# The pool groups of a two-layer decoder trunk: seven block products for eight in the looped groups, one weight sum by accumulating DMAs

## What is computed

```python
def pool_branch(xn, w_in, w_group, scale, w_out):
    u, g = jnp.split(xn @ w_in, 2, axis=-1)          # 2048 -> 2 x 4096
    for gi, w in enumerate((2, 4, 8, 16)):           # 4 groups of 1024 columns
        outs.append(windowed_mean(u[group gi], w) - u[group gi])
    mixed = einsum('bsgc,gce->bsge', stack(outs), w_group) * scale
    return (mixed * silu(g)) @ w_out                 # 4096 -> 2048
```

## Time and profile before

| what | value |
|---|---|
| median of the runs | 1543.48 us |
| profiled execution | 1544.08 us, its span 1542.0 us, granted clock 0.998 |
| busy in the span | PE 99%, DVE 72%, ACT 61%, POOL 2% |
| matmuls | 6788 records |
| DMA | 333.11 MB, 216 GB/s; queue of plain loads 60.7% and queue of POOL's DMAs 5.8% of 16 engines |

### The profile page before, as it was taken

The page is one execution under the profiler, slowest core; times in us unless marked ns, Lnnn a source line. Parts: engine busy times, 40 slices in busy tenths (PEclk is TensorE's granted clock), DMA queues, the critical chain, the costliest instruction groups (busy, mean ns, idle before and its releaser), DMA issues.

```text
span 1542.0 us, 19948 instructions
## 1 busy us (share of the span) xinstructions
PE 1525.7 (99%) x6788; PEld 1260.2 (82%) x6788; DVE 1114.2 (72%) x1382; ACT 935.8 (61%) x1124; POOL 28.9 (2%) x40
## 2 busy tenths in 40 slices
PE   9999999999999999999999999999999999999997
PEld 7887888888888888888888888888888888888885
DVE  6978787877878788887666675775577557755665
ACT  6466574657657574756777556644764476446853
POOL 0000000000000000000000000000000000000000
PEclk9999999999999999999999999999999999999999
DMA  9486786959678686965665757655765576555651
GB/s 382 167 257 222 223 239 218 244 171 276 220 217 244 218 219 223 242 224 198 223 220 187 219 211 219 217 196 191 218 219 189 194 221 228 210 208 180 223 195 72
DMA packets 137529, 333.11 MB, mean 216 GB/s; under 512 B 80992, under 2 KB 81008, under 8 KB 116368
## 3 DMA queue, kind: packets, MB, share of 16 engines
q1 hardware_dynamic: 132608, 314.35, 60.7%
q0 software_dynamic: 4736, 17.95, 5.8%
q10 hardware_dynamic: 144, 0.26, 0.0%
HBM read 312.08 MB, written 2.10 MB: 204 GB/s over the span
## 4 chain that ended last, share of the span: by engine, by line
PE 91%; DVE 3%; DMA 2%; issue 2%; ACT 2%; SPq 0%; ACTq 0%; POOL 0%; DVEq 0%; POOLq 0%
PE accA L515 11%; PE accA L517 11%; PE accA L516 11%; PE accC L515 10%; PE accC L517 10%; PE accC L516 10%; PE accB L515 6%; PE accB L517 6%; PE accB L516 6%; DMA w_raw<-in_stream_dram 2%; PE side L549 1%; PE side L548 1%; PE side L547 1%; DVE w_lo L1332 1%; PE accA L534 1%
## 5 line engine op out<-in xcount | busy, mean ns | idle before, releaser
L1332 DVE TENSOR_TENSOR w_lo<-w_raw,w_hi 128x1024 fp32r<-128x1024 f32 x326 | 395.8, 1222 | 226.3 <-ACT w_hi L861 224.6
L861 ACT CAST w_hi<-w_raw 128x1024 fp32r<-128x1024 f32 x326 | 340.0, 1052 | 263.2 <-PE accA L517 100.1
L1262 DVE TENSOR_TENSOR w_lo<-w_raw,w_hi 128x1024 fp32r<-128x1024 f32 (+1 forms) x280 | 320.9, 1167 | 95.4 <-ACT w_hi L874 95.4
L874 ACT CAST w_hi<-w_raw 128x1024 fp32r<-128x1024 f32 (+1 forms) x280 | 274.8, 1008 | 161.3 <-PE accA L517 79.4
L515 PE MATMUL accA<-w_hi,xa_hi 128*128 128x512 f32 x452 | 176.0, 389 | 0.8 <-DVE w_lo L1332 0.8
L517 PE MATMUL accA<-w_hi,xa_lo 128*128 128x512 f32 x452 | 175.9, 389 | 0.0
L516 PE MATMUL accA<-w_lo,xa_hi 128*128 128x512 f32 x452 | 175.9, 389 | 0.0
L515 PE MATMUL accC<-w_hi,xa_hi 128*128 128x512 f32 x396 | 154.3, 390 | 0.2 <-DVE w_lo L1262 0.2
L516 PE MATMUL accC<-w_lo,xa_hi 128*128 128x512 f32 x396 | 154.1, 389 | 0.0
L517 PE MATMUL accC<-w_hi,xa_lo 128*128 128x512 f32 x396 | 154.0, 389 | 0.0
L515 PEld LDWEIGHTS accA<-w_hi,xa_hi 128*128 128x128 f32 x452 | 84.8, 188 | 18.7 <-issue 1.1
(11 more groups left out here) (276 smaller groups left out, 2807.5 us busy)
## 6 DMA issues: line engine op xcount, KB each, us to landing
w_raw<-in_stream_dram SPq DMA_DIRECT2D x162, 1024.0 KB, 4.8
w_raw<-in_stream_dram SPq DMA_DIRECT2D x224, 512.0 KB, 5.5
w_raw<-in_stream_dram POOLq DMA_DIRECT2D x28, 512.0 KB, 8.6
h<-in_x_dram SPq DMA_DIRECT2D x4, 512.0 KB, 12.7
xT_raw<-in_xT_dram SPq DMA_DIRECT2D x3, 512.0 KB, 13.7
dec<-in_decay_dram POOLq DMA_DIRECT2D x1, 1024.0 KB, 9.1
fgain<-in_final_gain_dram POOLq DMA_DIRECT2D x1, 1024.0 KB, 7.5
out_dram<-emb SPq DMA_DIRECT2D x1, 1024.0 KB, 3.8
```

The lines of the kernel that those rows point to most:

```text
L861: act.copy(w_hi[:, r % RING, :], w_raw[:, r // 2, (r % 2) * 1024:(r % 2 + 1) * 1024]).then_inc(hi_ready, 1)
L874: act.copy(dst, unit_raw(name)).then_inc(hi_ready, 1)
L1262: dve.tensor_tensor(w_lo[:, u % RING, 0:n], unit_raw(ORDER[u]), w_hi[:, u % RING, 0:n].bitcast(F32), ALU.subtract).then_inc(lo_ready, 1)
L1332: dve.tensor_tensor(w_lo[:, r % RING, :], w_raw[:, r // 2, (r % 2) * 1024:(r % 2 + 1) * 1024], w_hi[:, r % RING, :].bitcast(F32), ALU.subt ...
```

## The change

In the looped groups, the first eight tiles of the two u products and of the two g products are done by the seven block products, with their own order (P_ORDER, 68 units: 40 whole ones and 28 parts), their own list of loads of 512 KB into named half-slots (P_LOADS), and the other work of ACT, DVE and SP at new places. u is the first pair, g the second. In pair u, T1 is made by DVE (pool_t1) and T3 by two accumulating DMAs; in pair g both T1 and T3 are made by accumulating DMAs. T2 and T4 are DVE's in both. POOL starts the sums of a group when the first turn's transposes have landed and T1 of u is there. The activation sums are made in group 0 (pool_form_sum, ACT's copies, pool_form_lo); f1 is written over a block of xa that is no longer used. In group 0 the two group products go to pairs B and C, not A and B, and the waits at the start of the last close change with them. The buffers of the snapshots and sums lie in parts of the arena and of other buffers. The stream is put in the order of the loads. Group 0 keeps its 40 units. The diff, cut to its core:

```diff
+P_ORDER = ("uA4 uM1a uA5 uM1b uA6 uM3a uA7 uM3b uC4 uM5a uC5 uM5b uC6 uM6a uC7 uM6b O0 uM7a O1 uM7b O2 uM4a O3 uM4b uM2a uM2b "
+           "O4 O5 O6 O7 O8 O9 O10 O11 O12 O13 O14 O15 gA4 gM1a gA5 gM1b gA6 gM3a gA7 gM3b gC4 gM5a gC5 gM5b gC6 gM6a "
+           "gC7 gM6b D0 gM7a D1 gM7b D2 gM4a D3 gM4b gM2a gM2b D4 D5 D6 D7").split()
...
+P_LOADS = (("uA4", 7, "uA4"), ("uX1a", 4, "uM4a"), ("uA5", 5, "uA5"), ("uX1b", 6, "uM4b"), ("uX2a", 2, "uM7a"), ("uA6", 0, "uA6"), ("uX3a",
+           1, "uM5b"), ("uA7", 3, "uA7"), ("uX2b", 7, "uM7b"), ("uX3b", 5, "uM6a"), ("uC4", 0, "uC4"), ("uC5", 3, "uC5"), ("uC6", 0, "uC6"),
+           ("uC7", 3, "uC7"), ("uX4a", 1, "uM2a"), ("uX4b", 0, "uM2b"), ("O0", 5, "O0"), ("O1", 3, "O1"), ("O2", 5, "O2"), ("O3", 2, "O3"),
+           ("O4", 3, "O4"), ("O5", 7, "O5"), ("O6", 5, "O6"), ("O7", 4, "O7"), ("O8", 2, "O8"), ("O9", 6, "O9"), ("O10", 1, "O10"), ("O11",
...
+P_TURNS = ('uX2b', 'uC6', 'O11', 'gA5')
...
+P_FORMS = (2, 0, 1, 3)
+FORM_SUM = (15, 33, 35, 36)
+FORM_HI = (17, 36, 38, 39)
+FORM_LO = (18, 37, 38, 39)
...
+            def group_loads(g, base):
+
+                last = {(POOL1 + r) % (2 * RAW): max(r, 1) - 2 * RAW for r in range(2 * RAW)}
+                for n, (name, b, last_name) in enumerate(P_LOADS):
+                    if name in P_TURNS:
+                        sp.wait_ge(halves_ready, g * 8 + (2 * POOL_TURNS - 4 + 2 * P_TURNS.index(name) + 2))
+                        sp.sem_inc(turn_begun, 1)
+                        transpose_halves(in_emb, halvesT_landed)
+                    sp.wait_ge(lo_ready, base + (last[b] + 1))
+                    last[b] = P_AT[last_name]
+                    at = g * (GROUP_U // (2 * RAW)) + ((POOL1 - GROUP_U + n) // (2 * RAW))
+                    s = (POOL1 + n) // 2 % RAW
+                    half = (POOL1 + n) % 2 * UNIT * COL
+                    sp.dma_start(slot(b), rounds[at, s, :, half:half + UNIT * COL]).then_inc(pool_landed[b], 16)
...
+            def add_pool_block(g, base, x, term, used):
+
+                n = POOL1 + [name for name, _slot, _last in P_LOADS].index(term)
+                at = (g - 1) * (GROUP_U // (2 * RAW)) + n // (2 * RAW)
+                half = n % 2 * UNIT * COL
+                pool.wait_ge(lo_ready, base + (P_AT[used] + 1))
+                pool.dma_start(slot(P_SLOT[x]), rounds[at, n // 2 % RAW, :, half:half + UNIT * COL],
+                               accum_op=ALU.add).then_inc(p_sum_landed[x], 16)
+
+            def group_sums(g, base, p):
+
+                if p == "g":
+                    add_pool_block(g, base, p + "X1a", p + "X2a", p + "M1a")
+                    add_pool_block(g, base, p + "X1b", p + "X2b", p + "M1b")
+                if p == "u":
+                    pool.wait_ge(p_t1_ready, g * 2)
+                wait_pool_landed(pool, g, p + "X2a")
+                add_pool_block(g, base, p + "X2a", p + "X3a", p + "M1b")
+                wait_pool_landed(pool, g, p + "X2b")
+                add_pool_block(g, base, p + "X2b", p + "X3b", p + "M1b")
...
+            for g in range(1, GROUPS):
+                base = g * GROUP_S + (POOL1 + MORE - GROUP_S)
+                pool.wait_ge(halvesT_landed, (POOL_TURNS + g * 4 - 1) * 16 * TT)
+                group_sums(g, base, "u")
+                group_sums(g, base, "g")
...
+            def pool_part(name, base, bank, hi, lo, first):
+
+                u = P_AT[name]
+                i = "ab".index(name[3])
+                pe.wait_ge(lo_ready, base + (u + 1))
+                for b in range(UNIT):
+                    j = i * UNIT + b
+                    wh = w_hi[:, u % RING, b * COL:(b + 1) * COL]
+                    wl = w_lo[:, u % RING, b * COL:(b + 1) * COL]
+                    pe.matmul(bank, hi[:, j, :], wh, start=first and j == 0, stop=False, skip_group_check=True)
+                    pe.matmul(bank, hi[:, j, :], wl, start=False, stop=False, skip_group_check=True)
+                    mm = pe.matmul(bank, lo[:, j, :], wh, start=False, stop=j == QUADS - 1, skip_group_check=True)
+                mm.then_inc(unit_used, 1)
...
+                pe.wait_ge(pg_ready, n2)
+                pool_a("u", 4, base)
...
+                pool_part("uM1b", base, side[0][:], *a11, False)
+                pool_a("u", 6, base)
+                pe.wait_ge(p_f_ready, FORMS)
+                pe.wait_ge(m_ready, n2)
+                pool_part("uM3a", base, acc["C"][0][:], *f4, True)
...
+                pool_c("u", 7, base)
+                pool_part("uM6b", base, side[0][:], *f2, False)
+                pe.wait_ge(mT_ready, n2)
+                mixed_out(0, base)
+                pe.wait_ge(p_snap_ready, g * 6 - 4)
+                pool_part("uM7a", base, side[0][:], *f3, False)
+                mixed_out(1, base)
+                pool_part("uM7b", base, side[0][:], *f3, False)
+                mixed_out(2, base)
+                pool_part("uM4a", base, acc["A"][1][:], *a22, False)
...
+            def group_hi(g, u, base):
+
+                name = P_ORDER[u]
+                act.wait_ge(unit_used, base + (u + 1 - RING))
+                if name[:3] == "uM5":
+                    act.wait_ge(p_t1_ready, g * 2 + ("ab".index(name[3]) - 1))
+                elif name[1:3] in DMA_SUM:
+                    act.wait_ge(p_sum_landed[name[0] + DMA_SUM[name[1:3]] + name[3]], g * 16)
+                elif name[1:3] in SUM_OF:
+                    done = PAIRS.index(name[0]) * SUMS + SUM_OF[name[1:3]] + "ab".index(name[3]) + 1
+                    act.wait_ge(p_t_ready, g * (2 * SUMS) + (done - 2 * SUMS))
...
+
+            def pool_snapshot(dst, used):
+                act.wait_ge(unit_used, used)
+                act.copy(dst[:], side[0][:]).then_inc(p_snap_ready, 1)
...
+                for u in range(GROUP_S):
+                    group_hi(g, u, base)
+                    if u == 0:
                         m_halves(n2 - 2, 0)
-                    if not first and u == KD_U - 2:
+                    if u == 5:
                         m_words(n2 - 2, g * KG - KG, 0, turn)
+                    if u == 6:
+                        m_hi(g * KG - KG, 0, turn)
+                    if u == 7:
                         m_halves(n2 - 1, 1)
-                    if not first and u == 2 * KD_U - 3:
+                    if u == 13:
                         m_words(n2 - 1, g * KG - KG // 2, 1, turn + 1)
...
+                    if u == 14:
+                        m_hi(g * KG - KG // 2, 1, turn + 1)
+                    for i, p in enumerate(PAIRS):
+                        if u == P_AT[p + "M1b"] + 5:
+                            pool_snapshot(p_snaps[i][0], base + (P_AT[p + "M1b"] + 1))
+                        if u == P_AT[p + "M6b"] + 3:
+                            pool_snapshot(p_snaps[i][1], base + (P_AT[p + "M6b"] + 1))
+                        if u == P_AT[p + "M7b"] + 3:
+                            pool_snapshot(p_snaps[i][2], base + (P_AT[p + "M7b"] + 1))
...
+                    if u == 25:
+                        act.wait_ge(p_c_fixed, g * 4 - 2)
+                        u_part(n2, "C", base + (P_AT["uC7"] + 1))
+                    if u == 29:
+                        act.wait_ge(p_a_fixed, g * 4 - 2)
+                        u_part(n2 + 1, "A", base + (P_AT["uM2b"] + 1))
...
+                    if u == 62:
+                        act.wait_ge(p_c_fixed, g * 4)
+                        pg_sigmoid(n2, "C", base + (P_AT["gC7"] + 1), False)
+                    if u == 67:
+                        act.wait_ge(p_a_fixed, g * 4)
+                        pg_sigmoid(n2 + 1, "A", base + (P_AT["gM2b"] + 1), False)
...
+            def pool_t1(g, i, base):
+                dve.wait_ge(lo_ready, base + (P_AT["uM1" + "ab"[i]] + 1))
+                wait_pool_landed(dve, g, "uX2" + "ab"[i])
+                x1 = slot(P_SLOT["uX1" + "ab"[i]])
+                dve.tensor_tensor(x1, x1, slot(P_SLOT["uX2" + "ab"[i]]), ALU.add).then_inc(p_t1_ready, 1)
...
+            def pool_t2(p, i, base):
+                dve.wait_ge(lo_ready, base + (P_AT[p + "M5" + "ab"[i]] + 1))
+                x1 = slot(P_SLOT[p + "X1" + "ab"[i]])
+                dve.tensor_tensor(x1, x1, slot(P_SLOT[p + "X3" + "ab"[i]]), ALU.add).then_inc(p_t_ready, 1)
...
+            def pool_t4(g, p, i, base):
+                dve.wait_ge(lo_ready, base + (P_AT[p + "M6" + "ab"[i]] + 1))
+                wait_pool_landed(dve, g, p + "X4" + "ab"[i])
+                x1 = slot(P_SLOT[p + "X1" + "ab"[i]])
+                dve.tensor_tensor(x1, x1, slot(P_SLOT[p + "X4" + "ab"[i]]), ALU.add).then_inc(p_t_ready, 1)
...
+            def pool_fix_w(snaps, at, done):
+                dve.wait_ge(unit_used, done)
+                dve.wait_ge(p_snap_ready, snaps)
+                own.mark(dve.tensor_tensor(at[1][:], at[1][:], side[1][:], ALU.subtract))
+                own.mark(dve.tensor_tensor(at[3][:], at[2][:], side[1][:], ALU.subtract))
...
+            def pool_fix_c(at):
+                own.wait()
```

(86 more changed lines are left out.)

378 lines of the change are left out of this document (258 added, 120 removed), and 5 rows, old and new, of the table P_LOADS.

## The result

The changed kernel takes 1551.17 us (median of seven runs, 1549.47 to 1555.85) against 1543.48 (1540.48 to 1544.08) beside it: the ratio is 1.0057, 95% interval 1.0043 to 1.007. It is slower by 0.6%, where 1538 was forecast. The profiled span grew by 7.0 us, from 1542.0 to 1549.0.

The account below looks back on a forecast made before the run. PE's own list was taken to bound the kernel: 1544.1 - 16.3 saved + 10.5 of stalls (3.5 us in each of three groups) = 1538.3, forecast as 1538 us, range 1529 to 1549.

Parts of the forecast that it names:

- what PE saves: Looped groups: 72 matmuls fewer over three groups at 0.2267 us each, 16.3 us; a group's floor is 146.9 us.
- everything hidden: Whole kernel with PE's saving and no stall: 1544.1 - 16.3 = 1527.8 us; the rival near it, 1528 to 1533, had 0.22.
- what DVE and ACT get: Looped group: DVE 129 of 146.9 us (88%), ACT 100 (68%); on average both fit.
- Group 0's forms: Group 0: activation sums and copies, some 10 us of DVE, counted at nothing because DVE idles 33 of 111 us.
- the place: First 17 units of a looped group: second turn right ahead of uC6's load delays O0, a 3.0 us stall.
- the length of the turn: Second turn in a looped group: two transposes take 2.7 us to issue, so uC6's load goes out at 15.9.
- L: Landing time of uC6's load after issue, taken as 6.6 us; O0 stalls for L - 3.6, from 0 to 4.8.
- the slow rival: Second turn: transposes take 5.4 us, uC6 lands at 27, O0 stalls 7.4 us; time 1551.5; chance 0.15.
- the unit that waits: Looped groups: PE waits before O0, wanted at 32.6 us but able to start at 29 + L.
- Elsewhere I find only small things: Rest of a looped group, such as D2's reload and DVE's lead behind the second mean: 0 to 1.5 us, taken as 0.5.
- The accumulates themselves are not late: Looped group: even at 13.5 us T3 is there at 26, and PE wants M7 at 35; no stall.

Follow-up runs that it names:

- one-accumulate: Changed kernel with one of the first pair's two T3 sums (X2a) made by DVE, the other (X2b) by its accumulating DMA: 1540.88 us, ratio 0.9987.
- no-accumulate: Changed kernel without accumulates in the first pair: T3 left out, 1531.78 us (ratio 0.9934), or made by two DVE sums, 1535.0 us (0.9945).

## Why the prediction was wrong, step by step

**Right: what PE saves.** 72 matmuls fewer, and without the first pair's accumulates the time fell to 1531.8 us, and to 1531.7 with the final gain's load moved as well, within 4 us of the 1527.8 worked out for everything hidden.

**Right: what DVE and ACT get.** DVE was put at 129 us a group and ACT at 100; they measure 126.5 to 128.3 and 97.4 to 99.2. Group 0's forms cost nothing.

**Right: the place.** The second turn ahead of uC6 is the narrow place, and ACT's second halves end at 942.6, 13.2 us after PE began uA4 (929.37), the figure of the prediction.

**Wrong: the step that failed is the length of the turn.** It was "13.2 + 2.7 = 15.9" for uC6's issue; measured is 950.84 - 929.37 = 21.5. The 2.7 came from a pair that had nothing beside it, although the same paragraph had the two accumulates go out "near 11.2 and 12.2", landing some 8.6 later, and so moving over the whole turn. They were charged to L, the landing of uC6, and to nothing else: L was taken as 6.6 and is 3.9 to 4.9 in the three groups. What is in flight was put on the load behind the transposes, and fell on the transposes. The one-accumulate and no-accumulate runs measure this term: 7.5 to 7.9, 4.5 to 5.6 and 2.6 to 3.8 us with two, one and none.

**Wrong: the argument against the slow rival.** That rival had uC6 issued at 18.6 and landed at 27, and named 26 as the point from which it decides; uC6 landed at 26.0, and the time is the 1551.5 of the rival within 0.4 us. It was given 0.15 because "uC5's load goes out at 10, well ahead of the second turn": only a load of SP right ahead was counted as able to slow the pair, as in the earlier trace rows, and not POOL's transfers. The trace of before held a sign: the heads' first turn, behind two accumulates issued 8 and 13 us ahead, takes 3.8 us and not 2.6, and in the heads' code the T3 accumulates wait for the landed transposes. That the two times agree so closely is partly luck, as the price was reached in another way: the rival had one stall of 7.4 us at O0, and the trace has 2.8 to 4.1 us at uC6 itself, then a slower clock in two groups and waits ahead of O0 and gC6 in the third.

**Wrong: the unit that waits.** The prediction went from uC6's landing straight to O0 and never set it against uC6's own start, 24.5. With its own durations, a landing at 26.0 gives 26.0 + 1.05 + 1.22 = 28.3, 3.8 us late; 3.67 were measured.

**Wrong by omission: the clock.** The sum has no term for it. Two of the three waits at uC6 were followed by 2.4 and 2.2 us more, as the following unit ran at the lower level; together with the 1.6 at gC6 that is some 6 us of the 23 lost. It is not shown that the time would be shorter by as much at the upper level: in the third group, where no matmul was slow at uC6, PE waits 2.02 us ahead of O0 instead.

**Wrong: "Elsewhere I find only small things".** The third group's wait ahead of gC6 was not looked for, since the final gain's load was nobody's step. The change did not touch that load's line. The run that moved it takes 1531.7 us against 1535.0, and its trace is without the wait of 2.02 us.

"The accumulates themselves are not late" held, since PE waits ahead of uC6, O0 and gC6 alone and none of them uses an accumulated sum. It was the wrong question: it is not when they arrive that counts, but what is issued while they move.

## What to carry to other kernels

A transfer that is moved to an idle queue isn't free: ask which DMAs are issued while it is in flight, and take the duration of those from a row with the same traffic beside them, not from a quiet one. Transposes issued by an engine in program order hold up every load behind them, so transfers that have time should go out behind a turn, not ahead of it. Two sums of 1.2 us on an engine some 87% busy were cheaper than the DMAs that spared them.
